# Three weight units at once on TensorE behind the split norms, and a third place for the halved SSM weights, in a two-block transformer kernel

## The reference, cut to what matters

```
h  = modulate(x, norm_mix_g[0], ...);  y = attention(h @ w_qkv) @ w_o;   x = x + g1 * y      # "norm 2", then qkv
h  = modulate(x, norm_ffn_g[0], ...);  x = x + g2 * swiglu(h)                                # "norm 3", then ffn0
h  = modulate(x, norm_mix_g[1], ...);  z, xbc, dt = split(h @ w_in)                          # "norm 4", then ssm_dt, ssm_in
     xbc = silu(conv3(xbc) + b);  y = bidirectional SSD(xbc, dt);  x = x + g1 * ssm_output(y, z)
h  = modulate(x, norm_ffn_g[1], ...);  x = x + g2 * swiglu(h)                                # "norm 5", then ffn1
out = rmsnorm(x, final_norm_g)
```

## Time and profile before

| | |
|---|---|
| median of 3 runs | 1677.86 us (1676.86 to 1682.76) |
| the profiled execution: its time / its span | 1676.07 us / 1674.2 us |
| instructions | 22685 |
| TensorE matmul busy | 1557.3 us, 93% of the span |
| VectorE busy / ScalarE busy | 746.9 us, 45% / 599.3 us, 36% |
| the chain that ended last, by engine | TensorE 83%, VectorE 6%, ScalarE 5%, DMA 3% |
| mean granted TensorE clock | 0.946 |

### The profile page before, as it was taken

How to read it: one execution, slowest core, us unless ns; L and a number is a source line. 1 busy time by engine, 2 the same in 40 slices (tenths; PEclk the granted TensorE clock), 3 DMA queues, 4 the chain that set the end, 5 groups by cost and what they waited for, 6 DMA issues and landing times.

```text
span 1674.2 us, 22685 instructions
## 1 busy us (share of the span) xinstructions
PE 1557.3 (93%) x9424; PEld 1288.7 (77%) x9424; DVE 746.9 (45%) x1208; ACT 599.3 (36%) x1126; POOL 206.0 (12%) x195
## 2 busy tenths in 40 slices
PE   7999999897979988999999998799999899899997
PEld 6887799574835566788888886578898688699996
DVE  6761125315146733423322332776754762255453
ACT  4342344224225633422122222542344460253342
POOL 2000384011000001011001102000000130111021
PEclk9799999797979999999999999899999898899998
DMA  7313554854200014122323231222352242645451
GB/s 231 139 51 126 198 187 162 322 222 187 101 1 1 26 50 159 68 93 91 132 76 101 69 121 61 101 99 85 119 178 74 97 157 79 230 170 188 176 172 43
DMA packets 36109, 206.84 MB, mean 124 GB/s; under 512 B 4952, under 2 KB 9480, under 8 KB 14888
## 3 DMA queue, kind: packets, MB, share of 16 engines
q1 hardware_dynamic: 33344, 200.11, 33.1%
q10 hardware_dynamic: 1848, 2.52, 0.8%
q0 software_dynamic: 816, 2.78, 0.5%
HBM read 202.76 MB, written 2.62 MB: 123 GB/s over the span
## 4 chain that ended last, share of the span: by engine, by line
PE 83%; DVE 6%; ACT 5%; DMA 3%; issue 1%; POOL 1%; SPq 1%; ACTq 0%; POOLq 0%; DVEq 0%
PE lin L1647 18%; PE lin L1648 17%; PE lin L1649 17%; PE lin L1630 7%; PE lin L1753 3%; PE aux L1982 2%; PE modp L1679 2%; DMA ring<-ada_in 2%; PE lin L2005 1%; PE lin L2160 1%; PE aux L1988 1%; ACT hn_hi L671 1%; ACT hn L672 1%; PE aux L1695 1%; PE aux L2077 1%
## 5 line engine op out<-in xcount | busy, mean ns | idle before, releaser
L592 DVE TENSOR_TENSOR w_split<-ring,w_split 128x1024 fp32r<-128x1024 f32 (+1 forms) x140 | 187.0, 1339 | 383.3 <-ACT w_split L587 383.2
L587 ACT ACTIVATE w_split<-ring 128x1024 fp32r<-128x1024 f32 (+1 forms) x140 | 158.4, 1134 | 479.4 <-PE lin L1649 402.5
L1647 PE MATMUL lin<-hn_hi,w_split 128*128 128x512 f32 (+1 forms) x864 | 304.7, 353 | 13.9 <-DVE hn_lo L879 11.9
L1649 PE MATMUL lin<-hn_hi,w_split 128*128 128x512 f32 (+1 forms) x864 | 301.1, 348 | 0.0
L1648 PE MATMUL lin<-hn_lo,w_split 128*128 128x512 f32 (+1 forms) x800 | 276.6, 346 | 0.0
L1647 PEld LDWEIGHTS lin<-hn_hi,w_split 128*128 128x128 f32 x864 | 165.0, 191 | 41.8 <-DVE hn_lo L879 12.0
L1649 PEld LDWEIGHTS lin<-hn_hi,w_split 128*128 128x128 f32 x864 | 165.7, 192 | 20.4
L1648 PEld LDWEIGHTS lin<-hn_lo,w_split 128*128 128x128 f32 x800 | 153.7, 192 | 16.8
L1647 PE MATMUL lin<-hn_hi,w_split_ssm 128*128 128x512 f32 (+2 forms) x392 | 135.0, 345 | 14.2 <-DVE w_split_ssm L592 8.0
L1648 PE MATMUL lin<-hid_split,w_split 128*128 128x512 f32 (+1 forms) x416 | 143.2, 344 | 0.0
L1648 PE MATMUL lin<-hn_lo,w_split_ssm 128*128 128x512 f32 (+2 forms) x392 | 133.9, 342 | 0.0
(11 more groups left out here) (376 smaller groups left out, 2562.0 us busy)
## 6 DMA issues: line engine op xcount, KB each, us to landing
ring<-ada_in SPq DMA_DIRECT2D x48, 1024.0 KB, 4.9
ring<-ssm_in_in SPq DMA_DIRECT2D x24, 1024.0 KB, 4.8
ring<-od_in_in SPq DMA_DIRECT2D x12, 1024.0 KB, 4.9
ring<-ffn0a_in_in SPq DMA_DIRECT2D x11, 1024.0 KB, 6.4
ring<-ffn0b_in_in SPq DMA_DIRECT2D x11, 1024.0 KB, 4.8
ring<-ffn1a_in_in SPq DMA_DIRECT2D x11, 1024.0 KB, 4.9
ring<-ffn1b_in_in SPq DMA_DIRECT2D x11, 1024.0 KB, 4.8
ring<-ev_in_in SPq DMA_DIRECT2D x9, 1024.0 KB, 13.5
```

The costliest lines, as they stand in the source:

```text
L587: act.activation(parts[:, 0], w, ACT.Copy).then_inc(sig("w_high"), 1)
L592: dve.tensor_tensor(parts[:, 1], w, parts[:, 0].bitcast(F32), ALU.subtract).then_inc(sig("w_low"), 1)
L1647: mm(lin[0:m, tile % RING, 0:width], hi, x_hi, start=kt == 0, stop=False)
L1649: ins = mm(lin[0:m, tile % RING, 0:width], lo, x_hi, start=False, stop=kt == kts - 1)
```

## The change

- **Three units together.** `split_together` waits for the banks and the low weights of three units, then, as each tile `kt` comes, issues the 9 matmuls of all three before it waits for the next. It is used for units 0 to 2 of qkv (norm 2), of ffn0a_in (norm 3) and of ffn1a_in (norm 5), and for `ssm_dt`, `ssm_in` 0 and 1 (norm 4). The matmuls and their number stay the same.
- **A third place** for the SSM projection's split weights, in memory that is used for other things only after it. `weights_hi` of unit u now waits for unit u - 3.
- **ScalarE's order.** The high part of `ssm_in` 1 moves into norm 4, before the root; units 2 and 3 follow the norm; in the loop, unit n + 4 (not n + 3) stands before the silu of n.
- **VectorE's order.** The low part of `ssm_in` 1 is made between the reciprocal and the scaling of norm 4. Units 2 and 3 come where 1 and 2 were, unit 4 within the softplus. In the loop `convolve` n now comes first, and the low part of unit n + 5 behind it.
- `linear` is written out without `rounds`; it issues the same instructions.

Cut to its core (definitions of the places, unchanged context and `linear` left out):

```diff
             if name[:3] == "ssm":
-                return "ssm_dt", w_split_ssm, 2, 0
+                return "ssm_dt", w_split_ssm, 3, 0
...
                 weights_hi(act, "ssm_dt", 0)
                 weights_hi(act, "ssm_in", 0)
+                weights_hi(act, "ssm_in", 1)
 
             act_norm(act, 4, 2 * L, "ffn0b_out", (1, 0, 2), True, first_weights)
-            weights_hi(act, "ssm_in", 1)
             weights_hi(act, "ssm_in", 2)
+            weights_hi(act, "ssm_in", 3)
...
             for n in range(48):
                 tile = lin_of["ssm_in"] + n
-                if n + 3 < 48:
-                    weights_hi(act, "ssm_in", n + 3)
+                if n + 4 < 48:
+                    weights_hi(act, "ssm_in", n + 4)
...
             dve.reciprocal(rcol[:, 0:width // P], rcol[:, 0:width // P]).then_inc(sig("rms"), 1)
+            if meanwhile is not None:
+                meanwhile()
             full(dve, "aux", tile + 1)
...
             weights_lo(dve, "ssm_dt", 0)
             weights_lo(dve, "ssm_in", 0)
-            modulated(dve, own, 4, 2 * L, 1, 0, 2)
-            weights_lo(dve, "ssm_in", 1)
+            modulated(dve, own, 4, 2 * L, 1, 0, 2, lambda: weights_lo(dve, "ssm_in", 1))
+            weights_lo(dve, "ssm_in", 2)
...
-            weights_lo(dve, "ssm_in", 2)
+            weights_lo(dve, "ssm_in", 3)
...
             own.link(tt(dt_tmp, dt_tmp, dt_tmp3, ALU.subtract))
+            weights_lo(dve, "ssm_in", 4)
             own.link(dve.reciprocal(da, da))
...
-            weights_lo(dve, "ssm_in", 3)
             dve.wait_ge(sig("ssm_in"), 32)
-            convolve(dve, own, 0)
-            convolve(dve, own, 1)
+            for n in range(2):
+                convolve(dve, own, n)
+                weights_lo(dve, "ssm_in", n + 5)
...
-            for n in range(2, 46):
-                weights_lo(dve, "ssm_in", n + 2)
+            for n in range(2, 43):
                 if n < 32:
                     convolve(dve, own, n)
+                weights_lo(dve, "ssm_in", n + 5)
                 if n == 4:
                     dve.wait_ge(sig("dt_weights"), 1)
...
+            def split_together(units, x, width, waits):
+
+                for name, u, m in units:
+                    begin("lin", lin_of[name] + u)
+                    pe.wait_ge(sig("w_low"), unit_of[name] + u + 1)
+                for kt in range(KT):
+                    pe.wait_ge(sig("hn_ready"), waits + kt + 1)
+                    x_hi, x_lo = x(kt)
+                    for name, u, m in units:
+                        parts, _, _ = unit(name, u)
+                        hi, lo = (parts[:, part, kt * m:(kt + 1) * m] for part in range(2))
+                        out = lin[0:m, (lin_of[name] + u) % RING, 0:width]
+                        mm(out, hi, x_hi, start=kt == 0, stop=False)
+                        mm(out, hi, x_lo, start=False, stop=False)
+                        ins = mm(out, lo, x_hi, start=False, stop=kt == KT - 1)
+                        if kt == KT - 1:
+                            fills(ins, "lin")
...
-            split_unit("ssm_dt", 0, KT, lambda kt: (hn_hi[:, kt, :], hn_lo[:, kt, :]), 2 * L, 2 * M_HEADS,
-                       ("hn_ready", KT * 4))
-
-            for tile in range(48):
+            split_together([("ssm_dt", 0, 2 * M_HEADS), ("ssm_in", 0, P), ("ssm_in", 1, P)],
+                           lambda kt: (hn_hi[:, kt, :], hn_lo[:, kt, :]), 2 * L, KT * 4)
+
+            for tile in range(2, 48):
```

More of the change, by code:

```diff
@@ L576, in unit @@
             first, memory, places_, shift = chain(name)
-            parts = memory[:, (unit_of[name] + u - unit_of[first] + shift) % places_, :, 0:cols]
+            place = (unit_of[name] + u - unit_of[first] + shift) % places_
+            parts = memory[place][:, :, 0:cols] if first == "ssm_dt" else memory[:, place, :, 0:cols]
             return parts, ring[:, b % RING, u % per_block * cols:(u % per_block + 1) * cols], b
@@ L871, in second_block_scalar, with normed @@
             act_norm(act, 6, L, "ffn1b_out")
-        def normed(dve, k, width, a, shifted=False, split=None):
+        def normed(dve, k, width, a, shifted=False, split=None, meanwhile=None):
             def low(kt):
@@ L958, in gated_add, with modulated @@
                 taken(dve, "lin", lin_of[name] + KT - 1 - n)
-        def modulated(dve, own, k, width, layer, chunk, split=None):
+        def modulated(dve, own, k, width, layer, chunk, split=None, meanwhile=None):
             own.link(dve.scalar_tensor_tensor(
@@ L1610, in linear @@
             def linear(name, stage, tiles, kts, rhs, width=L, m=P, norm=None, ready=None):
[L1612 to L1618, removed]
+                for n, b in enumerate(blocks_of[name]):
+                    pe.wait_ge(w_in[b % RING], (b // RING + 1) * 16)
                     for j in range(tiles):
[L1620 to L1623, removed]
+                        tile = lin_of[stage] + n * tiles + j
+                        begin("lin", tile)
@@ L1624, in one @@
                         for kt in range(kts):
                             at = (j * kts + kt) * m
[L1626 to L1630, removed]
+                            if n == j == 0:
+                                if norm is not None:
+                                    pe.wait_ge(sig("hn_ready"), KT * norm + kt + 1)
+                                if ready is not None:
+                                    ready(kt)
@@ L1631, in one @@
+                            ins = mm(lin[0:m, tile % RING, 0:width], ring[:, b % RING, at:at + m], rhs(kt),
                                      start=kt == 0, stop=kt == kts - 1)
                         fills(ins, "lin")
-                rounds(pe, count, one)
+            def split_together(units, x, width, waits):
[14 more added lines that the diff above has]
+                            fills(ins, "lin")
@@ L1650, in split_unit, with split_linear @@
                 fills(ins, "lin")
-            def split_linear(name, kts, x, width, waits=None):
-                for u in range(dict(SPLIT)[name]):
+            def split_linear(name, kts, x, width, waits=None, later=None, norm=None):
+                first = 0
+                if norm is not None:
+                    first = 3
+                    split_together([(name, u, P) for u in range(first)], x, width, KT * norm)
+                for u in range(first, dict(SPLIT)[name]):
                     split_unit(name, u, kts, x, width, waits=waits if u == 0 else None)
+                    if u == 3 and later is not None:
+                        later()
             ada_at = [0]
@@ L1955, in _ @@
             ada_groups(6)
-            split_linear("qkv", KT, lambda kt: (hn_hi[:, kt, :], hn_lo[:, kt, :]), 2 * L, ("hn_ready", KT * 2))
+            split_linear("qkv", KT, lambda kt: (hn_hi[:, kt, :], hn_lo[:, kt, :]), 2 * L, norm=2)
             pe.wait_ge(sig("at_in"), 48)
```

8 lines of the change are left out of this document (5 added, 3 removed).

## The result

| | before | after |
|---|---|---|
| median of the runs | 1678.92 us (1675.80 to 1686.16, 20 runs) | 1686.05 us (1679.74 to 1690.64, 20 runs) |
| ratio of the runs, 95% interval | | 1.0034 (1.0021 to 1.0047): 5.7 us slower (3.5 to 7.9) |
| the profiled execution, time / span | 1676.07 / 1674.2 us | 1687.40 / 1685.6 us |

The change makes the kernel slower by 0.34%, less than the 0.5% that the prediction took as the limit of a measurement; over 20 runs of each kernel the interval stays clear of zero. The ratio is that of the means; the medians lie further apart, 7.1 us. Predicted were 1685.7 us and +7.8 us.

What follows compares the result with a forecast made beforehand. TensorE was taken as the bound wherever weights and inputs are there. 1676.07 - 8.7 + 16.5 = 1683.9 us for a profiled execution, plus 1.8 for the median of the runs, gave 1685.7 us; range 1679 to 1694.

Steps and rivals of the forecast that it cites:

- Part 1: Behind norms 2, 3 and 5: three units together remove TensorE's idle time between tiles, gaining 4.5, 3.7 and 0.5, sum -8.7 us.
- The two ends: Bounds on the norms' gain: -9.8 us if the low clock lasts as in norm 2 everywhere, -6.7 if 2 us longer.
- Part 2: Norm 4: the high part of unit 1 before ScalarE's table load starts the norm 1.06 us later; its low part costs nothing.
- Part 3: SSM projection: each unit becomes one closed round between VectorE's and ScalarE's in-order queues; +16.5 us, bounds +10 and +19.
- the narrow round: SSM projection, narrow units: one round of VectorE and ScalarE takes 4.17 us against 2.86 on TensorE.
- the term for dt: Start of the SSM projection: dt comes later, +5.5 us from the shared TensorE, about 4 back, norm 1.06 late: +2.6 us.
- ScalarE's block: Start of the SSM projection: ScalarE's 7.23 us of exponentials stand between unit 7's high part and the silu of 3: +3.7 us.
- rounds 0 to 4: Start of the SSM projection: five rounds in which VectorE waits 1.75 us each, +8.75 us.
- The third place carries: Rival, SSM projection: three places and the longer lead remove the 5.07 us wait and slow clock; faster, 1659 us; chance 0.08.
- The delay is made good before the narrow units: Rival, SSM projection: wide units recover 0.27 us each, 4.9 us over some 18; same, about 1680 us; chance 0.10.
- The clock falls in the narrow stretch: Rival, narrow units: TensorE idle 1.3 us in every 4.2 drops to half speed; slower, 1699 us; chance 0.10.
- The signs that were named ahead: No gaps behind norms 2 and 3, qkv 4 to 5 us earlier, VectorE idle 1.7, ten narrow waits of 1.3, projection 14 to 19 longer.

Runs made afterwards that it cites:

- e1: Changed kernel with the SSM projection's places, orders and first unit as before, so three units together behind norms 2, 3 and 5 only: 1668.79 us, 0.9949 of before.
- e5: Kernel before plus only the third place for the SSM weights, both orders untouched: 1672.52 us, 0.9966 of before.
- e8: e1 plus the third place, both orders of the SSM projection as before: 1661.01 us, 0.9897 of before.
- e9: e8 with unit 0's convolution ahead of dt's softplus and the low parts of units 3 and 4 moved forward: 1659.34 us, 0.9897 of before.
- e3: Changed kernel, but VectorE makes the low part of unit n + 4, not n + 5, behind convolution n: 1664.86 us, 0.9918 of before.
- e7: Changed kernel, but behind norm 4 the dt unit runs alone, units 0 and 1 after it: 1683.26 us, 1.0036 of before.
- e2: Changed kernel with only the SSM part of the change, the other norms as before: 1697.83 us, 1.0099 of before.
- e4: Changed kernel, but ScalarE makes the high part of unit n + 5, not n + 4, ahead of the silu of n: 1665.22 us, 0.9927 of before.

## Why the prediction was right, point by point

**Part 1, norms 2, 3 and 5** (predicted -8.7). Norm 2: 72.65 - 68.60 = 4.1 us (4.5). Norm 3: from its first matmul to norm 4's it was 1045.74 - 669.55 = 376.19 and is 1042.98 - 670.47 = 372.51, 3.7 less although norm 4 starts 1.1 later, so 4.8 (3.7). Norm 5, to the end of the span: 208.9 to 208.1, 0.8 (0.5). The sum is -9.7; e1 has -8.6 in the whole. The terms were off by what was left open: the slow clock lasted 5.1 and 3.4 us, not 4.1 and 5.9. It isn't the same in each execution either: in e1, with the same code, it lasted 4.1 and 3.3 us. The two ends that the prediction gave this part don't follow from its own figures. With 4.1 us everywhere they give 4.5 + 4.5 + 1.3 = 10.3, not 9.8, and with 7.9 us everywhere 2.7 + 2.7 - 0.4 = 5.0, not 6.7; the measured 9.7 lies between in either case.

**Part 2** (+1.06). From norm 4's first matmul to the dt unit's first it was 1045.74 - 1038.42 = 7.32 us and is 1042.98 - 1034.55 = 8.43, +1.1. In e1, e5, e8 and e9, which have the old order of norm 4, it is 6.87 to 7.55 us, and in all kernels with the new one 8.42 or 8.43, so the term is 0.9 to 1.6 us. The high part explains 1.06 of it; that the low part beside TensorE cost nothing fits this, but had no run of its own.

**Part 3** (predicted +16.5 with part 2; measured 238.0 - 223.3 + 1.1 = +15.8). Steps: the narrow round 4.16 us (4.17 predicted); the wide one from 1114.14 to 1119.29, 5.15 (5.17). `convolve` 5 starts 71.2 us behind the first matmul (1114.14 - 1042.98), before 61.0 (1106.71 - 1045.74): 10.2 and the 1.1 of part 2, 11.3, where +12.45 was predicted. Most of that miss is the term for dt: L1100, the first instruction behind the exponentials, comes 24.8 us after the first matmul, before (L1094 at 1069.90) 24.2, so dt is 0.6 + 1.1 = 1.7 us later, not 2.6. ScalarE's block kept VectorE idle for 5.31 us where a plain round has 1.65, +3.7 as predicted; the other four of rounds 0 to 4 have 1.64 or 1.65 each, where 1.75 was counted. TensorE took the bank 0.80 us after L1008 began in a wide unit (1115.75 to 1116.55) and 0.54 in a narrow one, where 0.6 was estimated.

**The sum.** -9.7 + 15.8 = +6.1 us, against +7.8 predicted and +5.7 (3.5 to 7.9) measured. So the mechanism and its parts were right. That the median came within 0.4 us of 1685.7 is partly chance: both parts are 0.7 to 1.0 us off in the same direction, and before's own median is 1.1 us higher over 20 runs than over the three that the forecast started from. The two profiled executions differ by more, 11.3 us. Of that 1.3 us lie ahead of norm 2 and 3.3 us in the attention between qkv and norm 3, which the change doesn't touch; the last section shows why.

**The rivals.** *The third place carries* asked for rounds under 2.86 us in the narrow units; they were 4.16. With the round open (e3) its mechanism appears: 14 us faster, not the 19 that it priced, since the stall at unit 4 stays. *The delay is made good before the narrow units*: this did happen, at 5.16 us a round against TensorE's 5.44, and was just complete at unit 22 (see e7). Its price was wrong. It gave the stage +10 us, and the stage has +15.8, for two reasons. The narrow units alone cost 11.5, since the rounds of 22 and 23 still take 5.16 us while TensorE is already in units of 2.86. And TensorE had itself lost 4.3 us before that: 1.1 in part 2, the rest in the waits at the start and in a term that stood in no sum of the wide units, the clock. It is 0.81 and 0.83 where TensorE had waited 2.8 and 1.8 us, and 1.00 behind:

```profile
1107.00:1116.00 9.00, 7.30 (x24) 5.58 (x24) 7.06 (x18) 1.57 (x2) 0.00 (x0) 0.81 0.32 117
...
1116.00:1126.00 10.00, 9.45 (x34) 7.63 (x35) 6.60 (x8) 3.16 (x4) 0.00 (x0) 0.83 0.10 13
...
1126.00:1199.00 73.00, 73.00 (x323) 60.48 (x322) 48.66 (x58) 22.25 (x28) 0.00 (x0) 1.00 0.28 101
```

In the second of these rows the matmuls stand 0.43 us apart from 1117.97 to 1120.95, eight of them, 8 x 0.2 = 1.6 us. In the first they do so from 1108.06 to 1110.62, which is about as much. The forecast's own sum went through one chain of rounds and needed none of this: it had `convolve` 24 at 170.6 us behind the first matmul (1217.4 less 1045.74 + 1.06), and it came at 169.8 (1212.74 - 1042.98). *The clock falls in the narrow stretch* did not happen in the changed kernel either:

```profile
1209.00:1246.00 37.00, 27.62 (x213) 26.00 (x214) 23.25 (x35) 13.74 (x21) 0.00 (x0) 1.00 0.40 141
```

TensorE was busy for 27.62 of 37 us there, idle for a microsecond in each round, at a granted clock of 1.00. The rule of the Trainium skill that was weighed here ("TensorE: Matmul & The Clock Gate", the section on psum-queue depth-cycling) is not borne out by this stretch, nor by that of e7 (1.00 from 1210 to 1247 us). In e2, which has the same orders, the clock did fall there once. Its first narrow wait is 2.03 us, and soon behind it matmuls of 256 columns stand 0.21 us apart, until 1225.0 (TensorE, e2):

```profile
1221.03 0.38 PE L1664 MATMUL lin<-hn_hi,w_split_ssm 128*128 128x256 f32 x1 [2.03 <-DVE arena L1008]
...
1222.22 0.42 PE L1666 MATMUL lin<-hn_hi,w_split_ssm 128*128 128x256 f32 x1
```

The granted clock is 0.66 from 1221 to 1226 us and 1.00 again from 1226 to 1259, with idle times of 1.0 us in each round. The projection is 238.1 us long all the same: the unit after it no longer waits, and then the round sets the pace again. So this rival came in part in e2, without its price.

The signs that were named ahead came as well: no idle time in the 72 matmuls behind norms 2 and 3, qkv done 4.1 us earlier, the low parts late by 1.65 us behind the high parts, and L1664 waiting for L1008 some 1.0 to 1.3 us in narrow units, nine of them, 9.7 us in all, where ten were named.

## What to carry to other kernels

Ahead of a reordering across in-order queues, follow one item once around all of them: if every step stands behind the one before it, the sum of the latencies is the period, and idle time on each engine doesn't help. Compare that period with the shortest stage the order runs through, not with the average one; here the round was below the 5.44 us of a wide unit, so that a delay at the start was made good by only 0.3 us a unit, and it cost 1.3 us in each of nine narrow ones. A longer lead (n + 5 in place of n + 4) can be the slower choice when it puts a request behind the consumer of the step before: with the shorter lead the same three places gave a stage of 216.2 us, with the longer one 238.0.

## What the hardware showed that had not been expected

The same instructions of the attention take up to 12 us longer in one profiled execution than in another. The rows are 188 us from the first matmul behind qkv in four of the kernels, in all of which this part is the same, before, after, e4 and e7 (columns as in the earlier trace rows):

```profile
470.69:658.69 188.00, 166.99 (x786) 102.20 (x786) 104.87 (x220) 85.29 (x216) 8.53 (x7) 0.91 0.09 30
```

```profile
467.94:655.94 188.00, 170.49 (x785) 103.91 (x786) 102.89 (x217) 83.63 (x214) 7.72 (x6) 0.88 0.08 29
```

```profile
462.77:650.77 188.00, 170.62 (x740) 102.47 (x741) 101.36 (x214) 82.14 (x212) 6.44 (x5) 0.85 0.08 29
```

```profile
461.95:649.95 188.00, 170.61 (x722) 101.22 (x723) 100.55 (x213) 80.48 (x211) 5.15 (x4) 0.83 0.06 23
```

The granted clock is 0.91, 0.88, 0.85 and 0.83, and the way from there to norm 3's first matmul of the sum of squares is 188.6, 191.9, 196.9 and 201.0 us. The lower the clock, the longer the way, and the other seven traces fit in between (191.6 to 193.0 us at 0.88 or 0.89, 195.4 at 0.87, 196.9 at 0.85). The executions of one kernel differ by nearly as much (1675.80 to 1686.16 us before), so two profiles alone would have put this change at +11 us, and could have given a change of a few microseconds either sign. What was safe to compare were stages: the projection's length was 238.0 and 238.1 us in the two kernels that share it, and 223.3 and 223.4 in the two others, but 218.4 and 217.2 in e5 and e8, so a microsecond is not told apart there either. What makes the clock differ between executions was not tried.

Nor was it expected that a wait of 1.8 us is followed by a spell at the lower clock level (1117.97 to 1120.95, above), while in the narrow units idle times of 1.0 us in every 4.16 us left the clock at 1.00. The length of one wait doesn't settle it: in e1 TensorE waits 1.89 us before unit 4 (1084.86), and the clock is 1.00 from 1084.8 to 1103 us. Nothing here was tried to find out what does.
